# Stick-breaking attention on one core: the value product of tile c-3 issued directly behind the turn of tile c

## The reference, cut to what matters

```python
def stick_breaking(q, k, v, q_pos, k_pos):
    z = jnp.einsum('bqhd,bkhd->bhqk', q, k).astype(jnp.float32) * (HEAD_DIM ** -0.5)
    mask = k_pos[None, :] < q_pos[:, None]
    log_keep = jnp.where(mask, jax.nn.log_sigmoid(-z), 0.0)
    after = lax.cumsum(log_keep, axis=3, reverse=True) - log_keep
    w = jnp.where(mask, jnp.exp(jax.nn.log_sigmoid(z) + after), 0.0)
    return jnp.einsum('bhqk,bkhd->bqhd', w.astype(v.dtype), v)
```

## Time and profile before

| | |
|---|---|
| runs (median, lowest to highest) | 1672.51 us, 1667.76 to 1675.3 |
| the profiled execution's own time | 1670.41 us |
| its span, first to last instruction | 1668.6 us |
| mean granted TensorE clock | 0.934 of 2.4 GHz |
| busy: PE / DVE / ACT / POOL | 1459.9 / 1037.3 / 906.6 / 599.3 us |
| the chain that ended last, largest shares | PE 34%, issue 7%, POOL 4% |

### The profile page before, as it was taken

The page is one execution under the profiler, slowest core; times in us unless marked ns, Lnnn a source line. Parts: engine busy times, 40 slices in busy tenths (PEclk is TensorE's granted clock), DMA queues, the critical chain, the costliest instruction groups (busy, mean ns, idle before and its releaser), DMA issues.

```text
span 1668.6 us, 23809 instructions
## 1 busy us (share of the span) xinstructions
PE 1459.9 (87%) x7794; PEld 1218.4 (73%) x7794; DVE 1037.3 (62%) x1448; ACT 906.6 (54%) x1922; POOL 599.3 (36%) x495
## 2 busy tenths in 40 slices
PE   3639996898999999994589999999999999999989
PEld 3537774777777778773489879977788877777767
DVE  5316561655655656654356776678877889888841
ACT  7312222544454454442356666667777778787741
POOL 1000101120021020200244675556656576656742
PEclk9769998999999999997699999999999999999999
DMA  5561113344444343436595867756557565445543
GB/s 205 216 229 52 52 51 119 94 134 124 137 123 118 105 143 102 124 121 177 165 269 153 239 192 213 225 174 186 159 189 211 156 190 162 135 118 148 170 123 103
DMA packets 272926, 254.71 MB, mean 153 GB/s; under 512 B 26944, under 2 KB 195768, under 8 KB 272808
## 3 DMA queue, kind: packets, MB, share of 16 engines
q1 hardware_dynamic: 272808, 253.24, 49.6%
HBM read 168.20 MB, written 85.16 MB: 152 GB/s over the span
## 4 chain that ended last, share of the span: by engine, by line
PE 34%; issue 7%; POOL 4%; ACT 2%; DVE 2%; DMA 1%; SPq 0%; POOLq 0%; DVEq 0%; ACTq 0%
PE c_flow L1554 6%; PE c_flow L1556 6%; PE c_flow L1555 6%; PE c_turn L1521 5%; PE c_score L1509 3%; PE c_o L1534 3%; PE c_score L1510 3%; PE c_o L1535 3%; POOL c_weight L1316 2%; POOL f_w_lo L1321 1%; DMA c_o_in<-oT 1%; ACT c_take L1355 1%; DVE c_kept L1440 1%; POOL c_o_in L1328 1%; PE c_flow L1569 1%
## 5 line engine op out<-in xcount | busy, mean ns | idle before, releaser
L1316 POOL TENSOR_TENSOR c_weight<-c_take,c_kept 128x512 f32<-128x512 f32 (+2 forms) x320 | 305.8, 982 | 93.8 <-PE c_turn L1521 83.3
L1440 DVE TENSOR_TENSOR_SCAN c_kept<-c_keep,c_kept,c_score 128x513 f32<-128x513 f32 x192 | 245.3, 1277 | 44.1 <-ACT c_take L1355 36.5
L1448 DVE TENSOR_TENSOR c_w_lo<-c_turn,c_w_hi 128x512 fp32r<-128x512 f32 (+1 forms) x320 | 191.9, 600 | 91.0 <-ACT c_w_hi L1363 88.4
L1363 ACT ACTIVATE c_w_hi<-c_turn 128x512 fp32r<-128x512 f32 (+1 forms) x320 | 171.3, 536 | 132.2 <-PE c_turn L1521 128.1
L1554 PE MATMUL c_flow<-f_hi,f_w_hi 128*128 128x512 f32 (+1 forms) x640 | 236.0, 369 | 7.5 <-DVE f_lo L1474 5.9
L1321 POOL TENSOR_TENSOR f_w_lo<-f_w_raw,f_w_hi 128x1024 fp32r<-128x1024 f32 x64 | 153.7, 2402 | 223.2 <-ACT f_w_hi L1375 201.0
L1555 PE MATMUL c_flow<-f_lo,f_w_hi 128*128 128x512 f32 (+1 forms) x640 | 227.8, 356 | 0.0
L1556 PE MATMUL c_flow<-f_hi,f_w_lo 128*128 128x512 f32 (+1 forms) x640 | 227.8, 356 | 0.0
L1355 ACT ACTIVATE c_take<-c_score 128x512 f32<-128x512 f32 (+2 forms) x320 | 173.6, 543 | 30.7 <-POOL c_weight L1316 30.6
L867 PE MATMUL b_ps<-XH,w_w_hi 128*128 128x512 f32 (+1 forms) x480 | 186.8, 389 | 0.0
L248 POOL TENSOR_TENSOR w_w_lo<-w_w_raw,w_w_hi 128x1024 fp32r<-128x1024 f32 x18 | 43.0, 2390 | 398.4 <-ACT w_w_hi L243 398.4
(11 more groups left out here) (219 smaller groups left out, 2930.1 us busy)
## 6 DMA issues: line engine op xcount, KB each, us to landing
f_k<-k_parts SPq DMA_DIRECT2D x80, 256.0 KB, 3.7
f_v<-v_parts SPq DMA_DIRECT2D x80, 256.0 KB, 2.7
f_w_raw<-in_w_in SPq DMA_DIRECT2D x32, 512.0 KB, 4.3
f_w_raw<-in_w_out SPq DMA_DIRECT2D x32, 512.0 KB, 4.4
w_w_raw<-in_w_in SPq DMA_DIRECT2D x18, 512.0 KB, 5.0
x_rows<-in_x_prompt SPq DMA_DIRECT2D x4, 2048.0 KB, 10.0
xh_parts<-XH SPq DMA_DIRECT2D x4, 2048.0 KB, 14.6
xl_parts<-XL SPq DMA_DIRECT2D x4, 2048.0 KB, 19.7
```

Source lines behind the costliest of these rows:

```text
L1316: pool.tensor_tensor(weight[:, u.number % 2, j, 0:n], take[:, j, 0:n], kept[:, j, 1:n + 1], ALU.mult).then_inc(weighted, 1)
L1440: dve.tensor_tensor_scan(kept[:, j, down], keep[:, c % 2, down], score[c % 2][:, 0:1].to_broadcast([P, n]), above, ALU.mult, ALU.bypass).t ...
L1448: dve.tensor_tensor(w_lo[n][:, cols], turn_ps[c % 2][:, cols], f32(w_hi[n][:, cols]), ALU.subtract).then_inc(lo_ready, 1)
```

## The change

In TensorE's slot c, the value product of tile c-3 is issued directly behind the turn of tile c, ahead of the scores of tile c+8 and of the woven products. Nothing is added or removed, and the other engines' instructions are as they were.

```diff
@@ -1578,6 +1578,8 @@
             for c in range(SLOTS_ALL):
                 if c < SB_SLOTS:
                     turn(c)
+                if 0 <= c - 3 < SB_SLOTS:
+                    mix(c - 3)
                 if c + 8 < SB_SLOTS:
                     front(c + 8)
                 for p in pieces:
@@ -1587,8 +1589,6 @@
                                 flow_atom(p, nth)
                             else:
                                 flow_rows(p)
-                if 0 <= c - 3 < SB_SLOTS:
-                    mix(c - 3)
```

## The result

The changed kernel takes 1738.36 us (median; 1736.31 to 1740.77) against 1671.93 for the kernel before: a ratio of 1.0399, 95% interval 1.0371 to 1.0427. The forecast was 1724 in a range of 1702 to 1745. The profiled execution has a span of 1735.3 us, 66.7 more than before, and the same 23809 instructions.

The account below looks back on a forecast made before the run. The prediction took TensorE's own work as the bound, so added waits are time. From the profiled 1670.4 us, plus 46 for stalls at heads' ends, plus 13.6 for the clock, minus 5.6 absorbed, it forecast 1724, range 1702 to 1745.

Parts of the forecast that it names:

- The product's wait for the remainder: At the value product moved behind the turn: waiting for VectorE's remainder of its tile costs 0, since the turn already waits.
- The wait at the heads' ends: TensorE's wait for VectorE's `finish` before a head's first `mix`: less work in front, stalls grow 37 to 56 us, 46 taken.
- the 60 to 78: Predicted total of TensorE's stalls in us over the 31 heads' ends, against 22.4 before.
- the upper sum: Stalls at heads' ends with ScalarE's and GpSimd's delays as they lay: 78 us, a growth of 56.
- The clock: TensorE's clock falls behind long stalls in super-blocks 2 and 3: 8 times 1.7 us, 13.6; bounds 0 and 25.
- two in three of the twelve: Share of the 12 long stalls in super-blocks 2 and 3 taken to lower TensorE's clock: 8 falls, 13.6 us.
- a fall at each of the twelve: The skill's rule applied to the 12 long stalls of super-blocks 2 and 3: each lowers TensorE's clock, 20 us.
- What came back: TensorE's waits for scores, 11.2 us: half, 5.6, absorbed by the new stalls; bounds 0 and 11.
- Rival 1: Stalls at heads' ends grow by 46 us but TensorE's clock holds at 2.4 GHz: 1711 us; chance 18%.
- rival 3: VectorE paces super-blocks 2 and 3, so TensorE makes good its stalls there: 1673 us, not slower; chance 6%.
- Rival 2: Stalls at heads' ends grow by 56 us, clock falls at every long one, nothing comes back: 1751 us; chance 14%.

## Why the prediction was right, and where it was too small

*The product's wait for the remainder*, costed at nothing, is nothing: turns still wait 1.0 us for it (1.3 in the earlier trace rows).

*The wait at the heads' ends* was right in mechanism and in both places worked out: 2.67 reckoned and 2.66 measured in super-block 3, 1.78 and 1.77 in super-block 1. In all, 70.7 us plus 31 times 0.16 are 75.7, inside the 60 to 78, and the growth is 53 over the 22.4. I took 46, the middle, on the ground that part of ScalarE's and GpSimd's delays would shrink. The total lies near the upper sum, which had them as they lay. The runs with the heads' first products moved back (+6 us) and moved alone (+52) show that this is the place.

*The clock* is the term that was mis-sized most. I reckoned 8 falls at 1.7 us, 13.6. By the rows, the time lost is the length times what the clock falls short of 1.00: in after 98 x 0.03, 191 x 0.01, 250 x 0.06 and 303 x 0.04, together 32; before, 92 x 0.04, 190 x 0.01 and 220 x 0.01, together 8. The difference is 24. The run with filled waits tests it: by the same reckoning it has some 2 us of this loss left (194 x 0.01), 30 less than the changed kernel, and 26 us came back, so most of what the rows call lost is time. The number of falls was too low. In stretches of 12 us around the 31 heads' ends the granted clock of after is below 1.00 at 17; in the kernel before there are three such places, the first three of the earlier trace rows. That is 14 more, where I took 8. In super-blocks 2 and 3 a fall came with 11 of the 12 waits that show 2.5 us or more, and with two of 1.87 and 1.88. My "two in three of the twelve" was drawn from the four stretches of the earlier trace rows, of which one, the 3.85, holds two waits (1.14 and 2.71), and I gave the shorter waits none:

```profile
1160.00:1170.00 10.00, 6.88 (x29) 5.43 (x28) 5.46 (x7) 4.77 (x11) 7.99 (x8) 0.83 0.46 134
1224.00:1234.00 10.00, 8.12 (x38) 6.72 (x37) 6.66 (x9) 5.51 (x13) 4.88 (x5) 0.83 0.54 165
...
1529.00:1539.00 10.00, 7.50 (x31) 5.82 (x30) 6.92 (x9) 5.34 (x12) 6.17 (x6) 0.86 0.28 85
1605.00:1615.00 10.00, 7.50 (x32) 5.75 (x30) 6.16 (x9) 5.47 (x12) 5.06 (x5) 0.83 0.28 79
1645.00:1655.00 10.00, 7.20 (x40) 5.62 (x38) 8.69 (x11) 7.49 (x16) 9.63 (x9) 1.00 0.64 199
```

The waits in the second and in the last of these stretches:

```profile
1227.91 0.47 PE L1534 MATMUL c_o<-c_w_hi,f_v 128*128 128x512 f32 x1 [1.88 <-issue]
...
1646.00 0.47 PE L1509 MATMUL c_score<-f_k,f_q_hi 128*128 128x512 f32 x1 [0.30 <-ACT c_take L1355]
...
1650.00 0.47 PE L1534 MATMUL c_o<-c_w_hi,f_v 128*128 128x512 f32 x1 [2.50 <-issue]
```

The second stretch lost its clock behind one wait of 1.88 us; the last one, with 2.50 and 0.30, kept it. The rule of the Trainium skill that the prediction weighed (TensorE: Matmul & The Clock Gate, section "HAM oscillation — how this bites in real kernels": idle stretches between groups of matmuls bring the array back to half clock, and it is paid each time) points the right way here. Taken as the prediction took it, with a fall at each of the twelve, it gives 20, nearer to the measured 24 than my 13.6. The waits in that section's own example are longer than most of those here, and a wait of 2.50 us that kept its clock shows that not every one is paid.

*What came back* was put at 5.6 us of the waits for scores; 8.2 of the 11.2 went.

The terms as measured are 53, 24 and -8, 69 against the 66.7 by which the span grew. The sums of the two tables part the same growth without these terms: for about as many matmuls (4293 against 4288) TensorE is idle for 42.7 us more and busy for 25.2 more (761.1 against 735.8), together the 68 by which the stretch is longer (842 against 774). The predicted terms were 46, 13.6 and -5.6. Rival 1 (the clock holds) fell with the granted clock of after; rival 3 (VectorE paces the longer rows) fell too, since super-blocks 2 and 3 grew by 42 us where the counts of matmuls are the same. Rival 2 had the high sum for the waits and the falls nearly right, and erred in bringing almost nothing back.

## What to carry to other kernels

Before an instruction that waits is moved up in an in-order queue, list what lay in front of its wait: that work was the cover, and what falls behind the wait holds up the engines that it feeds. A rare case of a common instruction (here the first product of a head, 31 of 320) can carry the whole cost, so cost the rare waits apart, and if the rest of the move is worth having, leave those out of it and let the releaser move up in its own queue. Where TensorE is the bound, a wait of some two microseconds may cost up to 1.7 us more through the clock.

## What the runs showed of the hardware that was not expected

The granted clock does not hang on the length of a wait alone: in the rows above it fell to 0.83 over 10 us behind one wait of 1.88 us and stayed at 1.00 behind one of 2.50. What decides was not tested. Work that nobody needs can pay on TensorE: the kernel with filled waits, with more instructions and no wait removed, ran 26 us faster than the empty ones (1712.44 against 1738.36).
